# Latent attention: values of two heads in one product, probabilities scaled before they are turned, query rotation on GpSimd, and output splits at later heads

## The reference, cut to what matters

```python
def mla_mixer(h, pos, w_in, g_qa, w_qb, g_kva, w_kvb, g_q, g_k, w_o):
    ...
    q = (rms_norm(q_lat, g_qa) @ w_qb).reshape(B, S, MLA_HEADS, MLA_QK)
    kv = (rms_norm(kv_lat, g_kva) @ w_kvb).reshape(B, S, MLA_HEADS, MLA_NOPE + MLA_V)
    q = jnp.concatenate([q[..., :MLA_NOPE], rope(q[..., MLA_NOPE:], pos)], axis=-1)
    ...
    v = kv[..., MLA_NOPE:]
    q = rms_norm(q, g_q)
    k = rms_norm(k, g_k)
    o = dense_attention(q, k, v, MLA_QK ** -0.5)
    return o.reshape(B, S, MLA_HEADS * MLA_V) @ w_o

def dense_attention(q, k, v, scale):
    ...
        s = jnp.einsum('bqhd,bkhd->bhqk', qi, k, preferred_element_type=jnp.float32) * scale
        p = jax.nn.softmax(s, axis=-1).astype(v.dtype)
        return jnp.einsum('bhqk,bkhd->bqhd', p, v)
```

## Time and profile before

| | us |
|---|---|
| median of 3 runs | 1631.92 |
| lowest and highest run | 1628.33, 1631.93 |
| the profiled execution, whole | 1629.21 |
| its span in the trace | 1627.4 |
| PE busy | 1567.3 |
| DVE busy | 1126.9 |
| ACT busy | 813.4 |
| POOL busy | 123.4 |

### The profile page before, as it was taken

The page is one execution under the profiler, slowest core; times in us unless marked ns, Lnnn a source line. Parts: engine busy times, 40 slices in busy tenths (PEclk is TensorE's granted clock), DMA queues, the critical chain, the costliest instruction groups (busy, mean ns, idle before and its releaser), DMA issues.

```text
span 1627.4 us, 28848 instructions
## 1 busy us (share of the span) xinstructions
PE 1567.3 (96%) x12118; PEld 1470.6 (90%) x12118; DVE 1126.9 (69%) x1428; ACT 813.4 (50%) x1064; POOL 123.4 (8%) x107
## 2 busy tenths in 40 slices
PE   7999999999999999999998999999999999999998
PEld 6999989998999999999887989998999999789997
DVE  5797677776688768777577576666777756665554
ACT  5565444344555444444567454445455555454442
POOL 1060000000132000000011000000211202000000
PEclk9999999999999999999998999999999999999999
DMA  9775476667676537576533257665887655345652
GB/s 291 250 250 190 139 235 221 221 207 242 215 258 222 198 131 274 189 230 204 186 126 112 94 170 254 229 226 179 293 279 250 206 167 174 110 129 183 207 174 86
DMA packets 230497, 325.56 MB, mean 200 GB/s; under 512 B 7416, under 2 KB 195296, under 8 KB 230368
## 3 DMA queue, kind: packets, MB, share of 16 engines
q1 hardware_dynamic: 223304, 313.00, 57.5%
q10 hardware_dynamic: 7064, 10.71, 2.1%
HBM read 314.23 MB, written 9.45 MB: 199 GB/s over the span
## 4 chain that ended last, share of the span: by engine, by line
PE 80%; DVE 9%; ACT 4%; issue 3%; DMA 3%; POOL 1%; SPq 1%; DVEq 0%; ACTq 0%; POOLq 0%
PE bank L516 25%; PE bank L517 24%; PE bank L518 24%; DVE wlo L1583 2%; ACT whi L1122 1%; PE bank L559 1%; DMA raw<-in_w_ffn_in 1%; PE bank L930 1%; PE bank L914 1%; PE bank L730 1%; PE bank L945 1%; POOL rstd L1054 1%; DVE ada_raw L1603 1%; DMA lbias<-forget_sums 1%; PE bank L850 1%
## 5 line engine op out<-in xcount | busy, mean ns | idle before, releaser
L1583 DVE TENSOR_TENSOR wlo<-raw,whi 128x2048 fp32r<-128x2048 f32 (+1 forms) x241 | 547.4, 2275 | 226.8 <-ACT whi L1122 226.6
L1122 ACT ACTIVATE whi<-raw 128x2048 fp32r<-128x2048 f32 (+1 forms) x241 | 456.2, 1897 | 116.8 <-PE bank L518 77.9
L516 PE MATMUL bank<-hT_hi,whi 128*128 128x256 f32 x1728 | 493.7, 286 | 5.3 <-DVE hT_lo L1698 3.0
L517 PE MATMUL bank<-hT_lo,whi 128*128 128x256 f32 x1728 | 488.9, 283 | 0.0
L518 PE MATMUL bank<-hT_hi,wlo 128*128 128x256 f32 x1728 | 488.9, 283 | 0.0
L516 PEld LDWEIGHTS bank<-hT_hi,whi 128*128 128x128 f32 x1728 | 331.2, 192 | 11.6 <-issue 9.1
L517 PEld LDWEIGHTS bank<-hT_lo,whi 128*128 128x128 f32 x1728 | 331.4, 192 | 1.2
L518 PEld LDWEIGHTS bank<-hT_hi,wlo 128*128 128x128 f32 x1728 | 331.4, 192 | 0.0
L516 PE MATMUL bank<-whi,hT_hi 128*128 128x256 f32 (+1 forms) x944 | 273.0, 289 | 5.2 <-DVE hT_lo L1698 2.4
L517 PE MATMUL bank<-wlo,hT_hi 128*128 128x256 f32 (+1 forms) x944 | 268.5, 284 | 0.0
L518 PE MATMUL bank<-whi,hT_lo 128*128 128x256 f32 (+1 forms) x944 | 268.4, 284 | 0.0
(11 more groups left out here) (277 smaller groups left out, 1501.8 us busy)
## 6 DMA issues: line engine op xcount, KB each, us to landing
raw<-in_mlp_w SPq DMA_DIRECT2D x64, 1024.0 KB, 5.7
ada_raw<-in_ada_w SPq DMA_DIRECT2D x96, 512.0 KB, 6.5
raw<-in_w_in SPq DMA_DIRECT2D x44, 1024.0 KB, 5.4
raw<-in_w_ffn_in SPq DMA_DIRECT2D x44, 1024.0 KB, 5.3
raw<-in_dil_w_in SPq DMA_DIRECT2D x36, 1024.0 KB, 5.7
raw<-in_w_ffn_out SPq DMA_DIRECT2D x22, 1024.0 KB, 4.9
raw<-in_w_o SPq DMA_DIRECT2D x8, 1024.0 KB, 5.3
biasb<-head_bias ACTq DMA_DIRECT2D x16, 512.0 KB, 4.5
```

The lines of the kernel that those rows point to most:

```text
L516: pe.matmul(dst, lh, rh, start=start, stop=False)
L517: pe.matmul(dst, lh, rl, start=False, stop=False)
L1122: act.activation(view(whi[c % SPL], c), view(raw[c % RAW], c), ACT.Copy).then_inc(s_hi, 1)
L1583: dve.tensor_tensor(view(wlo[c % SPL], c), view(raw[c % RAW], c), view(whi[c % SPL], c).bitcast(F32), ALU.subtract).then_inc(s_lo, 1)
```

## The change

- Values: `head_out`, `turn_pair` and `scale_out` are gone. At every even i from 4, PE multiplies for two heads at once: the stationary operand is 64 columns of `Vm`, 256 columns of `PTm` stream past it, and the result has the 64 value columns of the one head on the upper and those of the other on the lower half of the partitions. That is the layout that the turn of the pair made before. The result goes to one of the five banks. `PTm` has four buffers instead of two.
- Scaling: DVE multiplies `Pm` by `rz` in place, right behind the inversion in `begin_head(i + 2)`, two operations of 128x256, and signals `s_pnm`. PE's turn of `Pm` waits for this signal instead of the one of the exponentials. The first inversions of the next layer's heads wait for `s_pnm` too.
- Rotation: the six operations of `rotate_queries(g)` are on GpSimd, ahead of the inverse roots of group g, each linked to the one before by a semaphore.
- Splits: QB 3 stays after head 3; MO 0 is split after head 7 instead of 4, MO 1 after 11 instead of 8, MO 2 after 13 instead of 10.

```diff
-            PTm = [sb(f"PTm{i}", [P, TT, S], at=ph) for i in range(2)]
+            PTm = [sb(f"PTm{i}", [P, TT, S], at=ph) for i in range(4)]
...
-        SPLIT_AT = {0: 4, 3: 5, 4: 6, 8: 7, 10: 8}
+        SPLIT_AT = {0: 4, 3: 5, 7: 6, 11: 7, 13: 8}
...
             def end_head(i):
                 if 2 <= i < MH + 2:
                     u = unitm(i - 2)
-                    pe.wait_ge(s_exp, 2 * u + 2)
+                    pe.wait_ge(s_pnm, 2 * (i - 2) + 2)
...
-                if 3 <= i < MH + 3:
-                    u = unitm(i - 3)
-                    emptied(pe, ("T", u))
-                    head_out(u, lambda kt, h=i - 3: Vm[:, kt, HD * h:HD * h + HD],
-                             lambda kt, t, pt=PTm[u % 2]: pt[:, kt, P * t:P * t + P], ((0, 1), (0, 1)))
-                if i >= 5 and i % 2:
-                    turn_pair(unitm(i - 5) // 2)
+                if i >= 4 and i % 2 == 0:
+                    pair = unitm(i - 4) // 2
+                    for h in range(2):
+                        emptied(pe, ("T", unitm(i - 4 + h)))
+                    bk = begin("a", ("OT", pair))
+                    for kt in range(TT):
+                        for h in range(2):
+                            at = i - 4 + h
+                            m = pe.matmul(bk[64 * h:64 * h + 64, 0:S], Vm[:, kt, HD * at:HD * at + HD],
+                                          PTm[unitm(at) % 4][:, kt, :], start=kt == 0, stop=kt == TT - 1)
+                    end(m, ("OT", pair))
...
+            def rotate_queries(g):
+                for t in range(TT):
+                    emptied(pool, ("QB", g, t))
+                if g == 0:
+                    pool.wait_ge(s_krope, 2)
...
+                link(pool.tensor_tensor(r4(0), a, cb, ALU.mult))
+                link(pool.tensor_tensor(r4(1), b, sbn, ALU.mult))
+                link(pool.tensor_tensor(r4(2), b, cb, ALU.mult))
+                link(pool.tensor_tensor(r4(3), a, sbn, ALU.mult))
+                link(pool.tensor_tensor(a, r4(0), r4(1), ALU.subtract))
+                pool.tensor_tensor(b, r4(2), r4(3), ALU.add).then_inc(s_roped, 1)
+
             for g in range(MH // HG):
+                rotate_queries(g)
                 rsqrt(TT * HG, rq[:, g, :])
                 rsqrt(TT * HG)
...
-                if i >= 5 and i % 2:
-                    at_high(unitm(i - 5) // 2, (i - 5) // 2)
+                if i >= 4 and i % 2 == 0:
+                    at_high(unitm(i - 4) // 2, (i - 4) // 2)
...
                     if i < 4:
                         dve.wait_ge(s_pn1, u - 1)
                     else:
-                        emptied(dve, ("O", u - 2))
+                        dve.wait_ge(s_pnm, 2 * (i - 4) + 2)
                     dve.reciprocal(rz[:, u % 2, :], zsum[:, u % 2, :]).then_inc(s_rz, 1)
+                    dve.wait_ge(s_rz, u + 1)
+                    for t in range(TT):
+                        dve.tensor_scalar(Pm[u % 3][:, t, :], Pm[u % 3][:, t, :], rz[:, u % 2, t:t + 1], None, ALU.mult)\
+                           .then_inc(s_pnm, 1)
...
             def end_head(i):
-                if 3 <= i < MH + 3:
-                    scale_out(unitm(i - 3))
-                if i >= 5 and i % 2:
-                    at_low(unitm(i - 5) // 2, (i - 5) // 2)
+                if i >= 4 and i % 2 == 0:
+                    at_low(unitm(i - 4) // 2, (i - 4) // 2)
...
                     query_sums(g + 2)
-                    rotate_queries(g + 2)
```

More of the change, by code:

```diff
@@ L202, in block_pair @@
             sqq, sqk = sb("sqq", [P, TT, HG * MQK], at=ph), sb("sqk", [P, TT, HG * MQK], at=ph)
-            rt = sb("rt", [P, 4, TT * HG * 16], at=ph)
+            rt, rtq = (sb(n, [P, 4, TT * HG * 16], at=ph) for n in ("rt", "rtq"))
             qTm, kTm = ([sb(f"{n}_{i}", [MQK, HG, S], at=ph) for i in range(2)] for n in ("qTm", "kTm"))
@@ L257, in block_pair @@
         s_bst, s_pn = sem("bias_staged"), sem("probabilities_normed")
-        s_pn1 = sem("forgetting_probabilities_normed")
+        s_pn1, s_pnm = sem("forgetting_probabilities_normed"), sem("latent_probabilities_normed")
         s_mods, s_kn, s_kev = sem("mods_ready"), sem("keys_normed"), sem("keys_evacuated")
@@ L587, in _ @@
             pe.wait_ge(s_const, 16)
[L589 to L599, removed]
             def ffn_down(key, c, accs, nf, hid0, halfway=idle):
@@ L1092, in _, with r4 @@
                 rsqrt(TT, rlat[:, n, :])
+            def rotate_queries(g):
[3 more added lines that the diff above has]
+                    pool.wait_ge(s_krope, 2)
+                q4 = q96[g % 2][:, :, :].rearrange("p t (h n) -> p t h n", h=HG)
+                a, b = q4[:, :, :, MNOPE:MNOPE + 16], q4[:, :, :, MNOPE + 16:MNOPE + 32]
+                cb = cosn[:, :, :].unsqueeze(2).broadcast_to([P, TT, HG, 16])
+                sbn = sinn[:, :, :].unsqueeze(2).broadcast_to([P, TT, HG, 16])
+                def r4(i):
+                    return rtq[:, i, :].rearrange("p (t h f) -> p t h f", t=TT, h=HG)
+                link(pool.tensor_tensor(r4(0), a, cb, ALU.mult))
[4 more added lines that the diff above has]
+                pool.tensor_tensor(b, r4(2), r4(3), ALU.add).then_inc(s_roped, 1)
             for g in range(MH // HG):
+                rotate_queries(g)
                 rsqrt(TT * HG, rq[:, g, :])
@@ L1489, in end_head @@
                     bt = full(act, ("T", u))
-                    act.activation(PTm[u % 2][:, :, :], bt[:, :].rearrange("p (a s) -> p a s", a=2), ACT.Copy)\
+                    act.activation(PTm[u % 4][:, :, :], bt[:, :].rearrange("p (a s) -> p a s", a=2), ACT.Copy)\
                        .then_inc(drain_sem(("T", u)), 1)
-                if i >= 5 and i % 2:
-                    at_high(unitm(i - 5) // 2, (i - 5) // 2)
+                if i >= 4 and i % 2 == 0:
+                    at_high(unitm(i - 4) // 2, (i - 4) // 2)
             def after_head(i):
@@ L1722, in begin_head_norm @@
                 unfinished.append((mean_square(ss[:, 1, 0:8], 8, HD), job, r, buf))
[L1724 to L1730, removed]
             def at_low(pair, k, dst=classed):
@@ L2116, in query_sums @@
                 norm_at[g] = mean_square(ss[:, 1, 0:8], 8, MQK)
[L2118 to L2121, removed]
             def key_sums(g):
@@ L2191, in _ @@
             query_sums(0)
-            rotate_queries(0)
             dve.wait_ge(s_rstd, latent_at + 1)
@@ L2199, in _ @@
             turn_keys(0)
-            rotate_queries(1)
             key_sums(1)
@@ L2241, in norm_probs @@
                     if n < 2:
-                        emptied(dve, ("O", u - 2))
+                        dve.wait_ge(s_pnm, 2 * (MH - 2 + n) + 2)
                     else:
```

## The result

| | before | after |
|---|---|---|
| median (4 runs each) | 1631.14 us | 1648.99 us |
| lowest and highest | 1628.33, 1631.93 | 1647.15, 1651.36 |
| profiled execution, its span | 1629.21, 1627.4 | 1651.36, 1649.6 |

The ratio is 1.0113 with a 95% interval of 1.0092 to 1.0135: 17.9 us slower. The forecast was 1644.0 with a range of 1631 to 1652, so the time lies in the range, 5.0 above the forecast.

A forecast was written before the change was run, and what follows sets the result against it. PE, busy 96% of the span, was taken as the bound. Terms -7.8, -5.9, +17.0, +5.0, +0.3 and clock +3.5 gave +12.1 on 1629.2, so 1641.3, as a median 1644 us; range 1631 to 1652.

The forecast's parts named there:

- Order on DVE, idle at splits: PE waits for DVE's scaling queued behind splits after heads 3, 7, 11 and 13: 17.0 us of new idle.
- Waits between: Between splits, PE waits for DVE's low part, maximum and scaling: 5.0 us more (3 to 6).
- Pair product: Values of two heads in one PE product: 0.94 us per pair instead of 1.91, 7.8 us less work.
- rival 3: The array halves don't overlap in the pair product: +6.3 us on PE, 1650 us; chance 0.06.
- Start: Rotation on GpSimd, queued ahead of rq and rstd, makes kn and the first scores 0.3 us late.
- rival 4: GpSimd's rotation is at its slow end, maxima 3.4 us late: +4 in all, 1648 us; chance 0.09.
- Clock: PE at half clock after idle stretches: about 11 us lost against 7.5 before, so +3.5 us.
- rival 2: Idle as computed, but PE's clock stays up: 1633 to 1636 us, no measurable change; chance 0.14.
- upper bound of 18.6: Upper bound on PE's half-clock loss, if all of it runs at half clock: 18.6 us.
- The sum: +8.6 us at unchanged clock losses, +3.5 for the clock: +12.1 us in total.
- Rival 1: The scaling is never late, so the 17.0 us of split idle vanish: -14 us, 1618 us; chance 0.14.
- the vanished kn idle: PE's idle before the normed keys kn, 1.72 and 3.71 us, goes as splits move away from the keys.

The follow-up runs named there:

- e1: The changed kernel with the inversion and scaling one head earlier on DVE, right behind the next head's maximum and ahead of every split: 1633.6 us.
- e3: The changed kernel with the rotation back on DVE, all else kept: 1649.4 us.
- e6: The changed kernel without the scaling multiplications of the latent heads, PE's turn waiting for the exponentials alone: 1629.3 us.
- g1: e1 with the pair's product on one of the three banks of projections and turns instead of the five of scores: 1631.9 us.
- g2: e6 with the pair's product on one of the three banks of projections and turns instead of the five of scores: 1632.1 us.
- h1: g1 with splits behind the next head's exponentials and scaling, key sums and norming one head earlier, first output split after head 9: 1633.4 us.
- e4: The kernel before the change with only the new split table: 1633.5 us.

## Why the prediction was right, and where it was not

- **Order on DVE, idle at splits (17.0).** Right in place, number and size (17.1), and e1 confirms it as the cause: moving the scaling ahead of the splits returns 15.4 of 17.9 us.
- **Waits between (5.0)** were 6.5, or 5.8 more than before, since the earlier trace rows were read as gapless where 0.29 and 0.43 stood near the end. The 1.65 before the turn of head 7, right behind a gap, has no term in the working. The 0.58 before half of a turn of keys, where none was forecast, ended with ACT's `sqq` and not with kn.
- **Pair product (0.94)** was 1.01; the halves overlap (a record costs 0.126, not 0.215), so rival 3 is out. It saves 7.2 instead of 7.8. PE's work in the stage fell by 5.6 only; where the other 1.6 went stays open.
- **Start (0.3)** was 1.3. The step that failed is the bound on the queue behind the rotation: contention was in view as a mechanism, but I applied it to the rotation's own operations alone, and it fell on `rstd` (0.70) and `kn` (0.25). The slow end of rival 4 (0.81 an operation) did not come, a step costs 0.54, and e3 shows no gain from taking the rotation back.
- **Clock (11 against 7.4).** The cost in the stage was 11.5, but that is in part luck: 1.7 and 1.7 were right, 3.3 stands where I had 4.5, and 4.8 where I had 3. The 2.2 behind the stage were left out because I had the last gap heal inside it. The clock did not stay up, so rival 2 is out. The upper bound of 18.6 was given without its working.
- **The sum.** By the traces the forecast was 6.8 low (18.9 against 12.1), by the medians 5.0 to 5.8. The terms are clock behind the stage 2.2, PE's work 2.2, start 1.0, waits and gaps 0.9, clock in the stage 0.6.
- **Rival 1 had the wrong price.** It said 1618 if the scaling were never late. e1 is that case, and took 1633.6. The -14 added up PE's saved work, the vanished kn idle and its clock loss as if PE bounded the stage. In e1, e6, g1 and g2 PE's total idle was 11.3 to 13.0 us wherever the waits stood. h1 shows that the key chain over ACT, DVE and POOL ends last in B, since B fell from 11.5 to 6.5 with that chain moved up. That the loop of split, maximum and exponentials ends last in C is read from h1's trace; no run takes the loop away. The same mistake made my expectations of e1, e4 and e6 too low by 12 to 22, 6 to 14 and 11 to 17 us.

What stays open: what share of C is the scaling's DVE time and what the added splits. C is 3.1 shorter in e6 than in e1, and 1.2 shorter in g2 than in g1; in both pairs the scaling is left out, but the inversions also stand one head later. e4, which has the new splits and the old values, has C 2.1 longer than before.

## What to carry to other kernels

When an operation is put between two engines that handed over directly, look first at what is already queued ahead of it on its own engine: one multiplication of 0.6 us cost 15 us here because a split of 4 us stood in front of it four times. Work taken from the busiest engine counts only up to the next chain; before crediting it, follow each loop of handoffs over the other engines (here 6.6 us per two heads against 3.6 on PE) and take the longer one. The Trainium skill ("Perfetto Trace Analysis", Optimization Strategies) advises to optimize the engines on the critical path for which an idle matmul engine waits. Here PE was 96% busy before the change, so the trace showed little of what would block it next; the traces with less work on PE did.

## What was not expected of the hardware

- A GpSimd operation that began while a DVE operation with two SBUF operands ran took longer by what was left of that operation less 0.14: an inverse root of 128x8 2.34 instead of 1.64 us, a 128x128 multiplication 1.06 instead of 0.46. An inverse root that had begun first took its 1.64.
- Filling idle with unread matmuls made a kernel 7.4 us faster (1649.0 to 1641.6), as the granted clock went from 0.984 to 0.991.
- With the same 11.3 us of idle on PE in the stage, half clock cost 9.9 us in g2 (one gap of 4.63, two of about 2) and 4.8 in e6 (none over 1.90). The medians were 1632.1 and 1629.3.
